# A two-layer decoder trunk: order of loads and split of work in the first projection stage

## The reference

```python
c_act = silu(c)
for l in range(2):
    mod = c_act @ w_ada[l] + b_ada[l]              # 6 * 1024 numbers
    sh1, sc1, g1, sh2, sc2, g2 = split(mod, 6)
    h = rms_norm(x, norm1_g[l]) * (1.0 + sc1) + sh1
    proj = h @ w_in[l]                              # conv parts, q, k, v, gate
    ... convolution mixer, retention, output projection, residual with g1
    h2 = rms_norm(x, norm2_g[l]) * (1.0 + sc2) + sh2
    x = x + g2 * (square(relu(h2 @ w_up[l])) @ w_down[l])
return rms_norm(x, final_g)
```

## Time and profile before

| | |
|---|---|
| Median of 3 runs | 1161.94 us (1161.89 to 1162.43) |
| The profiled execution's own time | 1161.66 us |
| Its span | 1159.8 us |
| TensorE busy | 1131.3 us, 98% of the span |
| VectorE busy | 863.9 us, 74% |
| ScalarE busy | 580.2 us, 50% |
| GpSimd busy | 172.1 us, 15% |
| First V matmul starts | 24.18 us |
| Last tile of the V projection starts | 46.79 us |

### The profile page before, as it was taken

The page is one execution under the profiler, slowest core; times in us unless marked ns, Lnnn a source line. Parts: engine busy times, 40 slices in busy tenths (PEclk is TensorE's granted clock), DMA queues, the critical chain, the costliest instruction groups (busy, mean ns, idle before and its releaser), DMA issues.

```text
span 1159.8 us, 19123 instructions
## 1 busy us (share of the span) xinstructions
PE 1131.3 (98%) x6682; PEld 1006.8 (87%) x6682; DVE 863.9 (74%) x1315; ACT 580.2 (50%) x981; POOL 172.1 (15%) x132
## 2 busy tenths in 40 slices
PE   4999999999999999999999999999999999999996
PEld 2788888998989989989998888889989989999896
DVE  6967898679788687685677688886897575675754
ACT  5655544247445454454444555434555454544632
POOL 4484010320000000000215800004000000000003
PEclk9999999999999999999999999999999999999999
DMA  9774334624353353433345433452334232232312
GB/s 350 308 290 146 127 109 145 218 74 141 132 161 114 126 162 127 141 117 105 128 152 210 179 112 127 146 213 95 119 100 128 85 107 99 90 126 73 103 60 74
DMA packets 47061, 162.87 MB, mean 140 GB/s; under 512 B 5536, under 2 KB 7712, under 8 KB 46752
## 3 DMA queue, kind: packets, MB, share of 16 engines
q1 hardware_dynamic: 47008, 162.18, 40.2%
HBM read 160.06 MB, written 2.10 MB: 140 GB/s over the span
## 4 chain that ended last, share of the span: by engine, by line
PE 93%; DVE 3%; ACT 1%; DMA 1%; issue 1%; SPq 1%; POOL 0%; POOLq 0%; DVEq 0%; ACTq 0%
PE ps L368 21%; PE ps L369 21%; PE ps L370 21%; PE ps L524 8%; PE ps L526 8%; PE ps L525 8%; PE ps L621 1%; PE ps L410 1%; DVE h_lo L1092 1%; DMA w_raw<-weights 1%; PE ps L604 1%; PE ps L411 1%; PE ps L412 1%; DVE x L1129 1%; DVE x L1157 0%
## 5 line engine op out<-in xcount | busy, mean ns | idle before, releaser
L1013 DVE TENSOR_TENSOR w_lo<-w_raw,w_hi 128x1024 fp32r<-128x1024 f32 (+1 forms) x190 | 225.5, 1188 | 179.8 <-ACT w_hi L701 178.1
L701 ACT CAST w_hi<-w_raw 128x1024 fp32r<-128x1024 f32 (+1 forms) x190 | 189.2, 997 | 77.2 <-PE ps L370 66.6
L368 PE MATMUL ps<-u_hi,w_hi 128*128 128x512 f32 (+1 forms) x576 | 211.5, 367 | 0.0
L369 PE MATMUL ps<-u_lo,w_hi 128*128 128x512 f32 (+1 forms) x576 | 210.9, 366 | 0.0
L370 PE MATMUL ps<-u_hi,w_lo 128*128 128x512 f32 (+1 forms) x576 | 210.6, 366 | 0.0
L368 PE MATMUL ps<-h_hi,w_hi 128*128 128x512 f32 (+1 forms) x528 | 194.4, 368 | 0.8 <-DVE h_lo L1092 0.8
L370 PE MATMUL ps<-h_hi,w_lo 128*128 128x512 f32 (+1 forms) x528 | 192.0, 364 | 0.0
L369 PE MATMUL ps<-h_lo,w_hi 128*128 128x512 f32 (+1 forms) x528 | 192.0, 364 | 0.0
L1603 POOL TENSOR_TENSOR ssum<-ssum,buf_a 128x256 f32<-128x256 f32 (+1 forms) x56 | 51.7, 923 | 774.2 <-ACT buf_a L729 771.5
L1157 DVE SCALAR_TENSOR_TENSOR x<-ps,mod,x 128x512 f32<-128x512 f32 (+1 forms) x168 | 105.4, 669 | 34.5 <-PE ps L370 34.5
L370 PEld LDWEIGHTS ps<-u_hi,w_lo 128*128 128x128 f32 x576 | 108.7, 189 | 17.6
(11 more groups left out here) (196 smaller groups left out, 2324.8 us busy)
## 6 DMA issues: line engine op xcount, KB each, us to landing
w_raw<-weights SPq DMA_DIRECT2D x200, 512.0 KB, 3.4
ada_raw<-ada SPq DMA_DIRECT2D x80, 512.0 KB, 4.9
arena<-ada SPq DMA_DIRECT2D x16, 512.0 KB, 15.2
x<-xT SPq DMA_DIRECT2D x2, 1024.0 KB, 6.8
tab<-tables SPq DMA_DIRECT2D x2, 1024.0 KB, 14.5
outT<-x SPq DMA_DIRECT2D x8, 256.0 KB, 2.3
tab<-tables SPq DMA_DIRECT2D x1, 512.0 KB, 15.3
ident<-identity SPq DMA_DIRECT2D x1, 64.0 KB, 2.0
```

What stands on the lines that cost most here:

```text
L368: nc.tensor.matmul(out, wh, hi, start=first, stop=False, skip_group_check=True)
L369: nc.tensor.matmul(out, wh, lo, start=False, stop=False, skip_group_check=True)
L701: nc.scalar.copy(w_hi[:, j, cols], w_raw[:, j, cols]).then_inc(w_hi_done, 1)
L1013: nc.vector.tensor_tensor(w_lo[:, j, cols], w_raw[:, j, cols], w_hi[:, j, cols].bitcast(F32), ALU.subtract).then_inc(w_lo_done, 1)
```

## The change

Only the start of layer 0 changes.

- x is stored in HBM with the partition first, so that a load of four tiles reads 8 KB in one piece per partition where it read four pieces of 2 KB.
- `c_col` and `ident` are loaded from ScalarE's queue and not from SyncE's. SyncE's queue becomes: x tiles 0 to 3, x tiles 4 to 7, the four V weights, `bia`, `par`, scale 0, shift 0, scale 1, shift 1, and then shift k, scale k.
- The spread of the norm is two matmuls of 256 tokens. The first waits for two of the four diagonals.
- The rest of V weight slot 0 is made on VectorE, right behind the sum of squares, and those of slots 1, 2 and 3 on GpSimd.
- ScalarE rounds slots 0, 1 and 2 ahead of the root, and slot 3 behind the diagonals.
- VectorE makes the shift of tile 1 as well as that of tile 0. GpSimd and ScalarE make those of tiles 2 to 7.
- The factor `gm` of tiles 2 to 7 is made on ScalarE, in one instruction, from a precomputed `sc_gain`, which VectorE makes with one small extra multiply.
- On VectorE the order becomes: reciprocal, scale 0, gain 0, shift 0, product 0, scale 1, gain 1, low 0, product 1, shift 1, scale 2, low 1, product 2, scale 3, low 2, and so on.

```diff
@@ SyncE
-            sp.dma_start(c_col[:, 0, :], c_cols).then_inc(c_in, 16)
-            sp.dma_start(ident[:], identity).then_inc(c_in, 16)
             def load_x(i):
-                sp.dma_start(x[:, 4 * i:4 * i + 4, :], xT[4 * i:4 * i + 4, :, :].rearrange("k p t -> p k t")
+                sp.dma_start(x[:, 4 * i:4 * i + 4, :], xT[:, 4 * i:4 * i + 4, :]
                              ).then_inc(x_in[i], 16)
...
             load_x(0)
+            load_x(1)
+            for j in range(SLOTS):
+                sp.dma_start(w_raw[:, j, :], weights[j, :, :]).then_inc(w_in[j], 16)
             sp.dma_start(bia[:], bias).then_inc(par_in, 16)
             sp.dma_start(par[:], params).then_inc(par_in, 16)
-            load_x(1)
             load_scale(0)
             load_shift(0)
-            for j in range(SLOTS):
-                sp.dma_start(w_raw[:, j, :], weights[j, :, :]).then_inc(w_in[j], 16)
-                if j == 1:
-                    load_scale(1)
-            for k in range(1, KT):
+            load_scale(1)
+            load_shift(1)
+            for k in range(2, KT):
                 load_shift(k)
-                if k + 1 < KT:
-                    load_scale(k + 1)
+                load_scale(k)
@@ TensorE
             mean_squares(0, 0, 0, TOKEN_TILES)
-            spread(0, 1, WHOLE)
             pe.wait_ge(c_ready, 2)
+            for half, at in enumerate(HALVES):
+                if half == 0:
+                    pe.wait_ge(first_diag, 1)
+                else:
+                    pe.wait_ge(norm_r, 2)
+                spreads = nc.tensor.matmul(ps[:, RMS, at], ones[:], ssum[:, at], start=True, stop=True)
+            spreads.then_inc(rinv_ps, 1)
@@ ScalarE
+            act.dma_start(c_col[:, 0, :], c_cols).then_inc(c_in, 16)
+            act.dma_start(ident[:], identity).then_inc(c_in, 16)
...
+            def first_gain(k):
+                act.wait_ge(sc_summed, k + 3)
+                nc.scalar.activation(gm[:, 0, k:k + 1], sc_sum[:, k:k + 1], ACT.Identity, bias=sc_gain[:, k:k + 1],
+                                     scale=par[:, C_G1 + k:C_G1 + k + 1]).then_inc(gm_ready, 1)
-            act.wait_ge(par_in, 32)
             first_split(0)
             first_split(1)
+            first_split(2)
             norm_root(0, 1, TOKEN_TILES)
...
-            first_split(2)
             first_split(3)
+            act.wait_ge(par_in, 32)
             first_high(0)
-            for k in range(1, KT):
+            first_high(1)
+            for k in range(2, KT):
+                first_gain(k)
                 first_shift(k)
                 first_high(k)
@@ VectorE
+            dve.wait_ge(w_hi_done, 1)
+            nc.vector.tensor_tensor(w_lo[:, 0, :], w_raw[:, 0, :], w_hi[:, 0, :].bitcast(F32), ALU.subtract
+                                    ).then_inc(w_lo_done, 1)
+            dve.wait_ge(par_in, 32)
+            nc.vector.tensor_scalar(sc_bias[:], bia[:, 1:2 * KT:2], 1.0, None, ALU.add).then_inc(sc_summed, 1)
+            dve.wait_ge(sc_summed, 1)
+            nc.vector.tensor_tensor(sc_gain[:], sc_bias[:], par[:, C_G1:C_G1 + KT], ALU.mult).then_inc(sc_summed, 1)
...
+            dve.wait_ge(norm_std, 1)
+            nc.vector.reciprocal(rstd[:], std[:]).then_inc(norm_r, 1)
             first_scale(0)
             first_gain(0)
+            first_shift(0)
+            first_product(0)
             first_scale(1)
             first_gain(1)
-            first_split(2)
-            first_product(0)
             first_low(0)
             for k in range(1, KT):
                 first_product(k)
+                if k == 1:
+                    first_shift(1)
                 if k + 1 < KT:
                     first_scale(k + 1)
-                    first_gain(k + 1)
                 first_low(k)
@@ GpSimd
-            first_split(0)
-            first_split(1)
-            first_split(3)
+            for j in range(1, SLOTS):
+                first_split(j)
             pool.wait_ge(c_ready, 2)
-            for k in range(1, KT):
+            for k in range(2, KT):
                 first_shift(k)
```

More of the change, by code:

```diff
@@ L167, in trunk @@
         sc_bias = sb("sc_bias", [P, KT])
+        sc_gain = sb("sc_gain", [P, KT])
         warm = sb("warm", [P, 1])
@@ L225, in trunk @@
         gm_ready = sem("gm_ready")
+        first_diag = sem("first_diag")
         xr_ready = sem("xr_ready")
@@ L776, in first_shift @@
             def first_shift(k):
-                act.wait_ge(sh_product, k)
+                act.wait_ge(sh_product, k - 1)
                 nc.scalar.activation(arena[:, 2 * k, :], arena[:, 2 * k, :], ACT.Identity,
@@ L798, in _ @@
                 diag = nc.scalar.activation(ssum[:, t * P:(t + 1) * P], ident[:], ACT.Copy, scale=rstd[:, t:t + 1])
+                if t == 1:
+                    diag.then_inc(first_diag, 1)
             diag.then_inc(norm_r, 1)
-            first_split(2)
             first_split(3)
+            act.wait_ge(par_in, 32)
             first_high(0)
-            for k in range(1, KT):
+            first_high(1)
+            for k in range(2, KT):
+                first_gain(k)
                 first_shift(k)
@@ L812, in _ @@
                         if l == 0:
-                            act.wait_ge(sc_summed, 7)
+                            act.wait_ge(sc_summed, 8)
                             act.wait_ge(sh_summed, 7)
@@ L1187, in _ @@
             for m in range(1, KT):
-                if m == 4:
-                    dve.wait_ge(par_in, 32)
-                    nc.vector.tensor_scalar(sc_bias[:], bia[:, 1:2 * KT:2], 1.0, None, ALU.add).then_inc(sc_summed, 1)
                 dve.wait_ge(x_squared, m + 1)
@@ L1205, in first_gain @@
             def first_gain(k):
-                dve.wait_ge(sc_summed, k + 2)
+                dve.wait_ge(sc_summed, k + 3)
                 nc.vector.tensor_scalar(gm[:, 0, k:k + 1], sc_sum[:, k:k + 1], sc_bias[:, k:k + 1],
@@ L1225, in first_low, with first_shift @@
                                                ).then_inc(xs_lo, 2)
[L1228 to L1232, removed]
+            def first_shift(k):
+                dve.wait_ge(sh_in[k], 16)
+                nc.vector.tensor_tensor_reduce(out=arena[:, 2 * k, :], in0=arena[:, 2 * k, :], in1=c_row,
+                                               scale=1.0, scalar=0.0, op0=ALU.mult, op1=ALU.add,
+                                               accum_out=sh_sum[:, k:k + 1]).then_inc(sh_summed, 1)
+                dve.wait_ge(sh_summed, k + 1)
+                nc.vector.tensor_scalar(mod[:, 2 * k:2 * k + 1], sh_sum[:, k:k + 1], bia[:, 2 * k:2 * k + 1], None, ALU.add
+                                        ).then_inc(sh_ready, 1)
+            dve.wait_ge(norm_std, 1)
+            nc.vector.reciprocal(rstd[:], std[:]).then_inc(norm_r, 1)
             first_scale(0)
             first_gain(0)
[L1236 to L1243, removed]
+            first_shift(0)
+            first_product(0)
             first_scale(1)
             first_gain(1)
-            first_split(2)
-            first_product(0)
             first_low(0)
@@ L1260, in _ @@
                         dve.wait_ge(sh_summed, 8)
-                        dve.wait_ge(sc_summed, 9)
+                        dve.wait_ge(sc_summed, 10)
                         dve.wait_ge(w_hi_done, SLOTS + j + 1)
@@ L1731 @@
     arrays = {
-        "xT": np.asarray(x)[0].T.reshape(KT, P, T),
+        "xT": np.asarray(x)[0].T.reshape(KT, P, T).transpose(1, 0, 2),
         "c_cols": cols(c),
```

## The result

The changed kernel takes 1167.42 us (median of 5 runs, 1167.26 to 1167.92), the kernel before 1161.89 (5 runs): 5.5 us slower, a ratio of 1.0047 with a 95% interval of 1.0035 to 1.0059. The forecast was 1159.7 with a range of 1157.4 to 1163.1. The profiled execution has a span of 1165.7 us against 1159.8.

The account below looks back on a forecast made before the run. TensorE, busy 98% of the span, was taken to bound the kernel, with room in its late V start. Gains of 2.64, 0.59 and 0.80 (4.03) less 1.8 for ident gave 2.2, so 1159.7 us, range 1157.4 to 1163.1.

Parts of the forecast that it names:

- the small operations on VectorE: Before the reciprocal: sc_bias and sc_gain take 0.2 us each, hidden by means and root; at most 0.1 if uncovered.
- ident's delay: At the start, ident on ScalarE's queue lands d later behind x, lost in full: d = 1.8 us, from 0.6 to 2.8.
- the second rival: ident lands behind both x loads at 8.5, d = 5.3, time 1163.2 us, slower than before; chance 0.17.
- The two thirds: Where ident's delay was set between 0 and 2.8 us: two thirds of the way, d = 1.8.
- The rule of whole packets in turn: Each DMA engine drains a packet, typically 9 to 17 descriptors, before switching queues; ident follows one x load or both.
- the forecast's own sum: Last V tile starts 4.03 us earlier by the three terms, less ident's delay of 1.8, giving a 2.2 us gain.
- First term: Start of the V projection: the first V matmul moves from 24.18 to 21.54, a gain of 2.64 us.
- Second term: Between V tiles 0 and 1: tile 1 is ready before needed, so the 0.59 us gap is gone.
- the later rise to the fast spacing: In tile 0, TensorE's clock was assumed to rise as late after the first V matmul; otherwise some 1.2 us lost.
- Third term: Six steady V tiles from tile 1: TensorE paces at 2.75 us each, 16.50 instead of 17.30, a gain of 0.80.
- 8 KB pieces: Loads of x: 1 MB in 8 KB pieces costs 2.5 us, not 3.0, so x lands 0.5 sooner after issue.
- Loads in the new order: First-stage loads: bia and par land at 13.8, nothing waits for a load; smallest margin 0.4 us (scale 0).

Follow-up runs that it names:

- e11: The kernel of e3 with sc_bias and sc_gain back behind w_lo of slot 0, bia and par still early; 1162.73 us.
- e3: The changed kernel with c_col and ident heading SyncE's queue, bia and par right behind x, sc_bias and sc_gain between the adds of the squares; 1159.42 us.
- e1: The changed kernel with c_col and ident back at the head of SyncE's queue, all else kept; 1162.37 us.
- e4: The changed kernel with x stored and loaded in 2 KB pieces as before, c_col and ident still on ScalarE's queue; 1166.38 us.
- e5: The kernel of e1 with sc_bias adding a one from a tile of ones instead of an immediate one; 1162.72 us.
- e9: The kernel of e3 with c_col and ident on ScalarE's queue and bia and par issued ahead of x on SyncE's; 1159.25 us.
- e2: The changed kernel with sc_bias and sc_gain made between the adds of the squares, loads as in the change; 1163.78 us.
- e6: The kernel before with only c_col and ident moved to ScalarE's queue; 1162.79 us.
- e8: The kernel of e3 with gm of tiles 2 to 7 made on VectorE again; 1159.60 us.
- e12: The kernel of e3 with x loaded in 2 KB pieces as before; 1160.05 us.
- e10: The kernel of e3 with c_col heading SyncE's queue and ident alone on ScalarE's, both ahead of x; 1158.93 us.

## Why the prediction was wrong

**The failed step: the small operations on VectorE.** "With sc_bias and sc_gain (0.2 each, as the reciprocal's row of 0.18) it ends at 14.7 to 15.4, hidden by the means and the root; uncovered it would cost at most 0.1." They took 2.31 and 2.26 and held the reciprocal back by 3.3 (23.99 against the root's end at 20.64). e11 against e3 measures it alone: 1162.73 - 1159.42 = 3.3 us, with the reciprocal 3.39 later. It may be off by some tenths: e11's profile has five slow matmuls more than e3's, and how many the other executions had is not known. The price came from a row of the same length of work but of another kind, a reciprocal. The row that showed the truth stood among: w_lo on VectorE at 19.76 took 1.96. I read it as 1.2 slowed down. GpSimd's subtract of that moment ended at 15.96 + 4.68 = 20.64, and 1.96 is 0.88 of being shut out until then and about 1.08 of work. Priced that way, an operation of this kind, however short, costs up to 2.3 us behind GpSimd's start. In all five profiles in which sc_gain stands beside the subtracts (the change, e1, e4, e5, e11) both operations end within 0.04 us of a subtract's end.

The Trainium skill (SBUF — State Buffer, section Who interferes with whom) says just this: VectorE and GpSimd share a pair of SBUF ports, taken as a lock for a whole instruction, "the other **fully blocks** (not throttle)"; a VectorE instruction takes it with two SBUF inputs or in a mode that uses both ports, which `tensor_scalar` can enter when its operands allow it and a reciprocal isn't listed for. The trace agrees: 2.31 and 2.26 for sc_bias and sc_gain, ending with GpSimd's instructions, 0.17 for the reciprocal behind them. It also agrees that who starts first goes through: w_lo on VectorE, started first at 18.33, took its 1.22, and GpSimd's subtract, started at 18.86, was the one drawn out (5.19 for two, against 4.68).

**The term that was mis-sized: ident's delay.** The mechanism was forecast, with d = 1.8 from 0.6 to 2.8. It was 5.48, the size that the second rival gave ("d = 5.3; exponential at 8.5"), at a chance of 0.17. The step that failed is "On a queue of its own ident can pass part of x": both loads landed ahead of it (5.75 and 8.5, ident at 8.7). The two thirds had no ground either, as the row of bia showed a load in line behind one other, in one queue. The size is what alternation piece by piece gives (26 pieces of each queue from 6.0 to 6.5 us). e1 measures it at 5.05 us in the time. That it is x ahead of ident, and not the other queue, is shown by e9. How the DMA engines share their turns in general was not settled: with the same order ident landed at 8.7 (the change) and at 6.3 (e2). The rule of whole packets in turn that the prediction cites from the Trainium skill (DMA: Bandwidth & Descriptors, section Queues, rings and completion order) gave one load or both as the possible waits, and both were seen. The trace of the change doesn't agree with it on how, as there single pieces took turns; in e4, where no piece of ident went from 3 to 5 us, it fits.

**The sum.** With the two true terms the forecast's own sum is 4.03 - 5.48 - 3.3 = -4.8, so 1161.9 + 4.8 = 1166.7, 0.7 short of the 1167.42 measured. The last V tile's 4.98 agrees with it. What is left lies outside the first stage. In the profiles 0.5 is the slow spread at the end. The other 0.4 belongs to the change: from the last V tile to the final spread it is 1106.36 us before and 1106.39 in e6, which keeps the old order of work, and 1106.73 to 1107.01 in the twelve profiles with the new one. Together with the slow spread it is why e3, 3.76 ahead at the last V tile, is only 2.8 ahead in its span. The prediction let the whole gain of the first stage through; no run shows why part is lost.

**First term (earlier start, 2.64): right.** e3 has its first V matmul at 22.02 against 21.54 forecast, with x issued 0.93 later than the forecast had it.

**Second term (gap before tile 1, 0.59): the gap went, the gain did not come.** In the change the later rise to the fast spacing ate it: tile 0 took 5.25 and not 4.72. The forecast had named this as an assumption. In e3 the fast spacing begins by the tenth matmul (26.00), 4.0 after the first, as in the kernel before.

**Third term (steady tiles, 0.80): right.** 16.40 for the tiles after tile 0, where 16.50 was forecast. e8 shows the cause, with 2.89 a tile again once VectorE's head start is used up. In e3 the gains moved are worth 0.37 of it at the last V tile; tiles 1 and 2 take 2.75 and 2.72 even in e8, by that head start, which the forecast had not counted.

**8 KB pieces (0.5 for 1 MB): right.** x tiles 0 to 3 landed 5.0 after issue, 5.8 before; e12 gives 0.6 us.

**Loads in the new order: right.** par landed at 14.2 (forecast 13.8); no scale row was waited for in the change. In e3, e10 and e12 the timeline shows GpSimd waiting 0.2 to 0.9 for a shift row, hidden.

## What to carry to other kernels

Before an instruction is placed on VectorE beside GpSimd, look for a row where the two overlap and ask whether its end falls on the other's end: a shut-out instruction of eight numbers cost as much here as one of a thousand, and the cure was to place it a few microseconds earlier. A small load on which a chain hangs belongs ahead of the large ones in issue time, whatever queue it is on; being issued 0.44 us behind them cost 5 us here. A gain at the start of a kernel need not arrive whole at its end: 0.4 of it was lost on the way. Where a cost can lie between far ends, the row next to it has to match in kind (the same ports, the same number of queues) and not only in size.

## What was not expected of the hardware

- ident, 64 KB, took 7.5 us from issue to landing when 1 MB was issued 0.44 ahead of it on the other queue, and 2.3 when it was issued 0.49 ahead of that MB (e9).
- sc_bias, 128x8, took 0.17, 1.97, 1.99 or 2.31 us, by how much of GpSimd's running subtract was left when it started.
- From 6.0 to 6.5 us in the change, one 512-byte piece of ident went for each 8 KB piece of x, 26 of each. In e4 no piece of ident went from 3 to 5 us.
- The time from the first V matmul to the fast spacing was 5.25 us in the change and 4.0 in the kernel before and in e3, with no gap in TensorE's work inside that stretch in any of them. Over all the profiles it lay between 2.70 (e6) and 6.11 (e2).
- The same final norm spread took 0.67 us in the profile before and 1.19 in that of the change and most others.
